# One encoder layer on one core: inverse norms turned into rows on chip, edge factors by memset, score and attention side by side

## The reference

```python
def reference(x, norm1_g, w_in, pool_w, pool_scale, q_norm_g, k_norm_g, sinks,
              w_out, norm2_g, w_up, w_down):
    B, S, _ = x.shape
    for l in range(DEPTH):
        h = rms_norm(x, norm1_g[l])
        proj = jnp.einsum('bsd,de->bse', h, w_in[l])
        u = proj[..., :POOL_WIDTH]
        q = proj[..., POOL_WIDTH:POOL_WIDTH + Q_WIDTH].reshape(B, S, N_Q_HEADS, HEAD_DIM)
        k = proj[..., POOL_WIDTH + Q_WIDTH:POOL_WIDTH + Q_WIDTH + KV_WIDTH].reshape(B, S, N_KV_HEADS, HEAD_DIM)
        v = proj[..., POOL_WIDTH + Q_WIDTH + KV_WIDTH:].reshape(B, S, N_KV_HEADS, HEAD_DIM)
        a = pool_mixer(u, pool_w[l], pool_scale[l])
        b = swa_sink_attention(q, k, v, q_norm_g[l], k_norm_g[l], sinks[l])
        x = x + jnp.einsum('bse,ed->bsd', jnp.concatenate([a, b], axis=-1), w_out[l])
        h2 = rms_norm(x, norm2_g[l])
        hid = jnp.square(jax.nn.relu(jnp.einsum('bsd,df->bsf', h2, w_up[l])))
        x = x + jnp.einsum('bsf,fd->bsd', hid, w_down[l])
    return x
```

## Time and profile before

| what | value |
|---|---|
| median of 3 runs | 887.9 us (887.42 to 890.06) |
| the profiled execution, its own time | 889.13 us |
| its span, first to last instruction | 887.3 us |
| TensorE (PE) busy | 864.1 us, 97% of the span |
| VectorE (DVE), ScalarE (ACT), GpSimd (POOL) busy | 539.1, 407.8, 265.2 us |
| mean granted clock of TensorE | 0.994 of full speed |

### The profile page before, as it was taken

One profiled execution on the slowest core, in us unless ns is written; L12 is line 12 of the kernel. 1 busy time (PEld: TensorE's weight loads), 2 busy tenths in 40 slices (PEclk: granted clock), 3 DMA queues, 4 the chain that ended last, 5 costly groups with the idle time before them and its releaser, 6 DMA issues.

```text
span 887.3 us, 10763 instructions
## 1 busy us (share of the span) xinstructions
PE 864.1 (97%) x4062; PEld 711.1 (80%) x4062; DVE 539.1 (61%) x733; ACT 407.8 (46%) x714; POOL 265.2 (30%) x190
## 2 busy tenths in 40 slices
PE   8797899999999999999999999999999999999998
PEld 7576688678888888888888888888888888888887
DVE  7547856775447766656667656465955464646463
ACT  7346435553225565555555555554333333333330
POOL 1314525201024123432223432002544004444440
PEclk9899999999999999999999999999999999999999
DMA  9362202354110264554344553689762454152522
GB/s 354 54 137 97 60 25 72 82 207 139 48 47 24 86 224 145 184 161 162 131 131 141 186 163 116 212 307 393 271 222 99 149 197 142 59 179 73 165 87 79
DMA packets 69012, 128.90 MB, mean 145 GB/s; under 512 B 4833, under 2 KB 21473, under 8 KB 68961
## 3 DMA queue, kind: packets, MB, share of 16 engines
q1 hardware_dynamic: 68672, 128.08, 43.6%
q10 hardware_dynamic: 288, 0.14, 0.1%
HBM read 90.45 MB, written 37.75 MB: 144 GB/s over the span
## 4 chain that ended last, share of the span: by engine, by line
PE 79%; DMA 7%; DVE 6%; ACT 4%; POOL 2%; issue 1%; SPq 1%; ACTq 0%; DVEq 0%; POOLq 0%
PE bank L1489 26%; PE bank L1490 26%; PE bank L1491 26%; DMA mem<-in_x_T 2%; DMA mem<-in_x 2%; DMA rinv_keep<-mem 1%; DMA d_raw<-in_w_down 1%; DVE ring L1195 1%; PE bank L1502 1%; ACT mem L666 1%; POOL mem L561 1%; DMA raw<-in_w_up 1%; PE bank L1633 1%; DVE h_set L1227 1%; PE bank L1616 1%
## 5 line engine op out<-in xcount | busy, mean ns | idle before, releaser
L1489 PE MATMUL bank<-b_op,s_op 128*128 128x512 f32 (+1 forms) x450 | 174.7, 388 | 0.3 <-DVE b_op L1238 0.3
L1491 PE MATMUL bank<-b_op,s_op 128*128 128x512 f32 (+1 forms) x450 | 174.6, 388 | 0.0
L1490 PE MATMUL bank<-b_op,s_op 128*128 128x512 f32 (+1 forms) x450 | 174.6, 388 | 0.0
L650 POOL TENSOR_TENSOR b_sum<-d_raw,d_raw 128x1024 f32<-128x1024 f32 x40 | 97.7, 2443 | 200.6 <-DVE b_op L1238 200.6
L1234 DVE TENSOR_TENSOR s_op<-s_in,s_op 128x1024 fp32r<-128x1024 f32 x56 | 74.8, 1336 | 124.6 <-ACT s_op L861 124.6
L861 ACT ACTIVATE s_op<-s_in 128x1024 fp32r<-128x1024 f32 x56 | 59.4, 1060 | 177.4 <-PE bank L1491 150.3
L1195 DVE TENSOR_TENSOR ring<-raw,ring 128x512 fp32r<-128x512 f32 x96 | 87.8, 929 | 32.8 <-ACT ring L809 31.8
L1489 PE MATMUL bank<-xs,ring 128*128 128x512 f32 x256 | 99.8, 390 | 0.1
L1490 PE MATMUL bank<-xs,ring 128*128 128x512 f32 x256 | 99.6, 389 | 0.0
L1491 PE MATMUL bank<-xs,ring 128*128 128x512 f32 x256 | 99.6, 389 | 0.0
L1489 PEld LDWEIGHTS bank<-b_op,s_op 128*128 128x128 f32 x450 | 84.5, 188 | 18.2 <-DVE b_op L1238 0.7
(11 more groups left out here) (152 smaller groups left out, 1434.7 us busy)
## 6 DMA issues: line engine op xcount, KB each, us to landing
s_in<-h_keep SPq DMA_DIRECT2D x56, 512.0 KB, 3.9
h_keep<-h_set SPq DMA_DIRECT2D x16, 1280.0 KB, 5.1
raw<-in_w_up SPq DMA_DIRECT2D x16, 1024.0 KB, 6.2
d_raw<-in_w_down SPq DMA_DIRECT2D x32, 512.0 KB, 7.7
mem<-in_x SPq DMA_DIRECT2D x16, 512.0 KB, 6.7
h_keep<-h_set SPq DMA_DIRECT2D x16, 512.0 KB, 3.9
mem<-in_x_T SPq DMA_DIRECT2D x8, 512.0 KB, 7.9
x_keep<-mem SPq DMA_DIRECT2D x8, 512.0 KB, 3.0
```

The costliest lines, as they stand in the source:

```text
L650: nc.gpsimd.tensor_tensor(out=b_sum[G % 2], in0=group_rows(qa, g), in1=group_rows(qb, g), op=op).then_inc(b_summed, 1)
L1489: nc.tensor.matmul(out_ap, lhs[HI], rhs[HI], start=first, stop=False, skip_group_check=chained)
L1490: nc.tensor.matmul(out_ap, lhs[HI], rhs[LO], start=False, stop=False, skip_group_check=chained)
L1491: return nc.tensor.matmul(out_ap, lhs[LO], rhs[HI], start=False, stop=last, skip_group_check=chained)
```

## The change

The column of inverse norms becomes a row without leaving the chip. GpSimd copies the four columns of a half, each along 128 columns, into rinv_row (`spread_rinv`); TensorE transposes the four blocks into the bank QT_B, so that each row of the bank holds the norms of the tokens (`turn_rinv`); ScalarE copies the bank back into rinv_row (`take_rinv`); VectorE's scale_u waits for that. The bank is the one that transpose_in uses, so turn_rinv(h) waits for evac_qk(1) or evac_qk(3) (q_T_ready 2 or 4), and transpose_in(2) and (4) wait for take_rinv. The eight stores, two loads and the HBM tensor go.

The edge factors are written by GpSimd with 30 memsets at the start; VectorE's nine instructions go. On TensorE, the step that stood between score(t+1) and attend(t) is moved behind attend(t) (for attend(1) and attend(5) ahead of the score) at five places. split_w_out(4) is moved back on ScalarE and VectorE, and add_x1(0) is moved ahead of softmax_tail(7) on VectorE.

```diff
@@ -47,7 +47,6 @@
     w_down_i = w_down[0].rearrange("(j i p) n -> i p j n", i=2, p=P)
-    rinv_keep = nc.dram_tensor("rinv_keep", [2, NT // 2, P], F32, kind="Internal").ap()
     x1_keep = nc.dram_tensor("x1_keep", [NT, P, D], F32, kind="Internal").ap()
@@ -180,6 +179,7 @@
         TOK_B = [2, 3, 4, 0]
+        RINV_BEFORE = (2, 4)
@@ -193,7 +193,7 @@
         w_out_in = [sem(f"w_out_in{i}") for i in range(3)]
-        rinv_kept, rinv_row_in = sem("rinv_kept"), sem("rinv_row_in")
+        rinv_spread, rinv_turned, rinv_row_ready = sem("rinv_spread"), sem("rinv_turned"), sem("rinv_row_ready")
         stored = sem("stored")
@@ -333,17 +333,6 @@
                 sp.dma_start(w_u_stage[j], w_u_pair[j][:, :, 0:POOL_W]).then_inc(w_u_in[j], 16)
-
-            def turn_rinv(t):
-                sp.wait_ge(rinv_ready, t + 1)
-                sp.dma_start(rinv_keep[t // KH, t % KH].rearrange("(p i) -> p i", i=1), rinv[:, t:t + 1]).then_inc(rinv_kept, 16)
-
-            def load_rinv_row(h):
-                sp.wait_ge(rinv_kept, 16 * KH * (h + 1))
-                if h:
-                    sp.wait_ge(u_ready, GROUPS)
-                sp.dma_start(rinv_row, rinv_keep[h:h + 1].rearrange("h t p -> h (t p)").to_broadcast([P, HALF])).then_inc(
-                    rinv_row_in, 16)
@@ -413,30 +402,22 @@
             load_x(2)
-            turn_rinv(0)
-            turn_rinv(1)
             load_xT(3)
...
             load_xT(4)
-            turn_rinv(2)
             load_x(4)
-            turn_rinv(3)
             sp.wait_ge(w_u_lo, KT)
...
             sp.wait_ge(w_qkv_lo, KT + 1)
-            load_rinv_row(0)
             load_x(5)
...
                 load_x(t)
-            for t in range(4, NT):
-                turn_rinv(t)
             sp.wait_ge(xT_lo, 2 * (NT - 1))
...
             load_w_out(1)
-            load_rinv_row(1)
             sp.wait_ge(mix_done, GROUPS)
@@ -532,9 +513,10 @@
             pool.wait_ge(setup_pool, 5)
-            nc.gpsimd.iota(edge, [[0, GROUPS], [1, HALO]], base=1, channel_multiplier=0,
-                           allow_small_or_imprecise_dtypes=True).then_inc(setup_pool, 1)
-            pool.wait_ge(setup_pool, 6)
+            for g, w in enumerate(WINDOWS):
+                for j in range(w - 1):
+                    nc.gpsimd.memset(edge[:, g, j:j + 1], w / (j + 1)).then_inc(setup_pool, 1)
+                nc.gpsimd.memset(edge[:, g, w - 1:HALO], 1.0).then_inc(setup_pool, 1)
@@ -544,6 +526,15 @@
                                         op=ALU.pow).then_inc(rinv_ready, 1)
+
+            def spread_rinv(h):
+
+                pool.wait_ge(rinv_ready, KH * (h + 1))
+                if h:
+                    pool.wait_ge(u_ready, GROUPS)
+                column = rinv[:, KH * h:KH * (h + 1)].rearrange("p (t a) -> p t a", a=1)
+                nc.gpsimd.tensor_copy(rinv_row.rearrange("p (t n) -> p t n", n=P),
+                                      column.to_broadcast([P, KH, P])).then_inc(rinv_spread, 1)
@@ -602,6 +593,7 @@
             inverse_rms(3)
+            spread_rinv(0)
             head_squares(2)
@@ -613,6 +605,7 @@
             inverse_rms(7)
+            spread_rinv(1)
             window_sums(0, 3)
@@ -764,6 +757,10 @@
                                      scale=k_gain).then_inc(keys_ready, 1)
+
+            def take_rinv(h):
+                sc.wait_ge(rinv_turned, h + 1)
+                nc.scalar.activation(rinv_row, bank[QT_B][:, :], ACT.Copy).then_inc(rinv_row_ready, 1)
@@ -899,6 +896,7 @@
             evac_probs(0)
+            take_rinv(0)
             x_high(5)
@@ -922,6 +920,7 @@
             evac_probs(2)
+            take_rinv(1)
             copy_kv(4)
@@ -950,12 +949,12 @@
             copy_q(7)
-            split_w_out(4)
             evac_probs(5)
...
             pooled_high(1, 3)
+            split_w_out(4)
             attention_high(5)
@@ -1085,7 +1084,7 @@
                 dve.wait_ge(u_done, n + 1)
-                dve.wait_ge(rinv_row_in, 16 * (h + 1))
+                dve.wait_ge(rinv_row_ready, h + 1)
                 if h:
@@ -1097,6 +1096,8 @@
                 if h == 0:
+                    if g == 0:
+                        dve.wait_ge(setup_pool, 5 + sum(WINDOWS))
                     nc.vector.tensor_copy(u_T[:, g, 0:HALO], u_T[:, g, HALF:UB]).then_inc(halo_ready, 1)
@@ -1249,7 +1250,7 @@
-            dve.wait_ge(setup_pool, 6)
+            dve.wait_ge(setup_pool, 5)
             steps = [0]
@@ -1265,16 +1266,6 @@
                                                  scalar2=None, op0=ALU.mult))
-
-            def window_edges():
-
-                for g, w in enumerate(WINDOWS):
-                    step(nc.vector.tensor_scalar(out=edge[:, g, :], in0=edge[:, g, :], scalar1=float(w), scalar2=None,
-                                                 op0=ALU.min))
-                step(nc.vector.reciprocal(edge, edge))
-                for g, w in enumerate(WINDOWS):
-                    step(nc.vector.tensor_scalar(out=edge[:, g, :], in0=edge[:, g, :], scalar1=float(w), scalar2=None,
-                                                 op0=ALU.mult))
@@ -1309,7 +1300,6 @@
             place_values(1)
-            window_edges()
             head_sums(1)
@@ -1404,8 +1394,8 @@
             attention_low(6)
+            add_x1(0)
             softmax_tail(7)
-            add_x1(0)
             normed_x1(0)
@@ -1571,12 +1561,23 @@
                 pe.wait_ge(qk_ready, t + 1)
+                if t in RINV_BEFORE:
+                    pe.wait_ge(rinv_row_ready, RINV_BEFORE.index(t) + 1)
                 for pr in range(PAIRS):
...
                 nc.tensor.transpose(keys_bank(t), qkv[:, Q_W:Q_W + P], ident).then_inc(kT_done, 1)
+
+            def turn_rinv(h):
+
+                pe.wait_ge(rinv_spread, h + 1)
+                pe.wait_ge(q_T_ready, RINV_BEFORE[h])
+                for i in range(KH):
+                    tok = slice(i * P, (i + 1) * P)
+                    last = nc.tensor.transpose(bank[QT_B][:, tok], rinv_row[:, tok], ident)
+                last.then_inc(rinv_turned, 1)
@@ -1647,30 +1648,30 @@
             transpose_probs(0)
+            turn_rinv(0)
             project_u(0, 1, range(5, KT))
             score(1)
-            project_qkv(3, range(1))
             attend(0)
-            project_qkv(3, range(1, KT))
+            project_qkv(3, range(KT))
             transpose_in(2)
...
             score(2)
-            project_qkv(4, range(1))
+            project_qkv(4, range(2))
             attend(1)
-            project_qkv(4, range(1, 3))
+            project_qkv(4, range(2, 3))
             mix(0, 0)
...
             transpose_probs(2)
+            turn_rinv(1)
             project_qkv(4, range(6, KT))
             score(3)
-            project_qkv(5, range(0, 1))
             attend(2)
-            project_qkv(5, range(1, 4))
+            project_qkv(5, range(4))
             mix(0, 2)
@@ -1688,18 +1689,16 @@
             score(5)
-            project_qkv(7, range(1))
             attend(4)
-            project_qkv(7, range(1, 6))
+            project_qkv(7, range(6))
             transpose_in(6)
...
             transpose_probs(5)
-            project_out(0, range(0, 1))
+            project_out(0, range(0, 2))
             score(6)
             attend(5)
-            project_out(0, range(1, 2))
             mix(1, 2)
```

## The result

The changed kernel takes 872.9 us in the median (871.32 to 872.97, 4 runs), the kernel before 887.73 in the same comparison: a ratio of 0.9823, 95% interval 0.9803 to 0.9843, so 15.7 us less by these ratios. The forecast was 873.5 us, 869 to 879.5.

What follows compares the result with a forecast made beforehand. TensorE, busy 864.1 of 887.3 us, was taken to bound the kernel. The terms summed to 15.1 us, less 0.6 for small waits 14.5: 874.6 us for a profiled execution, 873.5 against the median, range 869 to 879.5.

Steps and rivals of the forecast that it cites:

- why xT(3) is late: Load of x_T's fourth tile: stands behind two 0.5 KB stores that slow everything queued behind them, and takes 11.2 us.
- xT(3) and the first wait: TensorE before 41.78: xT(3) lands in 5 us, so 5.59 us of idle time and 1.73 us of slow clock go.
- Next in line, 1.47 us: TensorE's wait before 58.07: loads and exponentials(0) come earlier, score(1) asks at 49.6, and 1.47 us go.
- The new way of the row: GpSimd's copy takes 1.06 us (bounds 0.5 and 2.1); two turn_rinv on TensorE cost 1.1 us.
- the rival of a held TensorE: TensorE waits 2 to 4 us at turn_rinv(0) for a late release: 877 us, chance 0.13.
- Score(1) to attend(1), 2.83 and 2.21 us: TensorE's waits before 76.86, 78.57 and 89.23: x(5) is issued earlier, so 2.83 and 2.21 us go.
- The third softmax: TensorE's waits of 0.80 and 2.15 us before 98.50 and 101.30: 2.4 us stay, 0.5 us won.
- The half clock: TensorE from 101.30 to 105.47: 1.4 us lost to slow clock, counted at one half, 0.7 us won.
- Adjacent score and attention, 0.8 us: TensorE, five places with a step between score and attention: 0.2 us a place won, four places counted, 0.8 us.
- split_w_out(4) and add_x1(0): Moving split_w_out(4) removes 0.35 us before score(6), w_out(7) landing 4 to 5 us later; add_x1(0) gives nothing.
- The rival of slow loads: xT(3) takes its 11.2 us whatever stands before it, only issued 1.45 us sooner: 881 us, chance 0.10.
- those of no change and of slower: Gain given back between 110 and 200 us: 887 us, chance 0.03; turn_rinv(0)'s wait grown: 891 us or more, 0.02.

Runs made afterwards that it cites:

- e1_word_stores_kept: The changed kernel with the eight stores of 128 neighbouring 4-byte words put back, read by nobody: 886.96 us against 889.8 of the kernel before.
- e2_wide_stores: The changed kernel with eight stores at the old places and with the old waits, each of 128 pieces of 512 bytes: 872.79 us, ratio 0.9806.
- e12: The changed kernel with the eight stores put back as 128 pieces of 64 bytes next to each other: 873.5 us against 890.1 of the kernel before.
- e13: The changed kernel with the eight stores put back as single words 64 bytes apart in HBM: 873.2 us against 888.8 of the kernel before.
- e8_step_between: The changed kernel with TensorE's old order, one step between score and attend, at the five places: 871.95 us, ratio 0.9823.
- e7: The changed kernel with pooled(0,2) moved on VectorE from behind softmax_head(2) to behind softmax_tail(2): 870.32 us, ratio 0.9779.
- e3_row_alone: The kernel before with only the new way of the row, without the edge-factor and order changes: 874.56 us against 889.8, ratio 0.9825.
- e10_tail_reordered: As e7, with attention_low(4) and softmax_head(5) of the first key head moved ahead of head_norm(6) on VectorE: 868.32 us, ratio 0.9757.

## Why the prediction was right, point by point

*What bounds the kernel, and why xT(3) is late.* Right: e1_word_stores_kept shows that the stores alone do it, e2_wide_stores that SyncE's wait, the place in the list and the number of pieces don't. One reading went too far: that the slow landings agree with a rule by the size of the piece. That rule is the Trainium skill's ("DMA: Bandwidth & Descriptors", Specifications): under 512 B a read-modify-write. e12 and e13 show that pieces under 512 bytes, down to single words, cost nothing that can be seen when no two share 64 bytes. The size alone doesn't give this case's times (873.2 to 873.5 us, against 872.8 with 512-byte pieces and 887.0 with neighbouring words); the measurement decides. The rival's rule (the Trainium skill, same page, "Why small descriptors are slow (HBM only)": only a small fixed cost a packet) describes the words apart and not the neighbours. What the chip does inside with neighbouring words was not seen, and whether it is the shared 64 bytes or the short stretch of the whole store stays open.

*xT(3) and the first wait.* Landing was put at 5 us and took 4.7. The 5.59 us went. The clock's share was called 1.73 and was 2.3: from 36.15 to 45.57 the same work took 9.42 us, where I had counted 9.97. Two slips made the difference. transpose_in's five transposes take 0.46 us, as the rows at 36.15 and 36.61 show, not 0.87, which is what the eight of transpose_probs take (45.57 to 46.44). And 0.87 and 39 times 0.228 are 9.76, not 9.97.

*Next in line, 1.47 us.* Right: exponentials(0) and the loads came as said, score(1) at 49.04 where 49.6 was forecast.

*The new way of the row.* GpSimd's copy took 0.61 us, inside the bounds of 0.5 and 2.1. turn_rinv took, by the chain of waits, 0.44 us at full clock (behind 46.44) and 0.76 at half (behind 85.78), 1.2 for both against 1.1 said. Neither waited, so the rival of a held TensorE, put at 0.13, didn't come.

*Score(1) to attend(1), 2.83 and 2.21 us.* Right: both waits are gone, attend(1) at 75.50 where 76.4 was said.

*The third softmax.* Of 0.80 and 2.15 us, 0.5 was expected to go; 0.80 went. The half clock was counted as half gone. In the profiled execution it came in full: the stretch behind the pause took 4.70 us (85.78 to 90.48) where the same work took 3.13 us at full clock (88.67 less 85.54 in e8_step_between). The mean clock was 0.998 in three of four runs of the changed kernel, so nearly nothing of the 0.7 us came. That the products beside GpSimd's sums are the cause was argued there and is shown by e7 for 3.0 of the 3.5 us. The Trainium skill says that GpSimd shares its SBUF interfaces with VectorE and contends with its two-input instructions ("GPSIMD Engine Reference", Specifications). The traces agree: 0.69 us alone, 1.42 and 1.62 beside the sums.

*Adjacent score and attention, 0.8 us.* Wrong, by the count. The 0.2 us a place is there, but of the five places only three put score and attention side by side (attend(0), attend(2), attend(4)), and I took off only the one ahead of 163.67, attend(4). The one at attend(0) lies before a wait that VectorE sets and is lost in it. One is left: from score(3) to the next transpose of keys 12.43 us (90.48 to 102.91) where it was 12.63. So 0.2 us came of 0.8.

*split_w_out(4) and add_x1(0).* The 0.35 us before score(6) went (no wait at 156.49), and nothing was late for the moved split. The changed kernel also has one step more ahead of score(6), but e8_step_between hasn't, and has no wait there either; e3_row_alone, with neither, has the 0.35 us. So the moved split is enough.

*The sum.* The terms as measured in the two profiled executions: 5.59 + 2.28 + 1.47 + 2.83 + 2.21 + 0.80 + 0 + 0.2 + 0.35 - 1.2 = 14.5, against 16.2 of the two spans. Of the other 1.7 us, 0.45 came between transpose_in(2) and score(2), beyond the two waits that went there (the distance of the two timelines grows from 9.22 to 12.50), and 0.3 between the transposes of keys at 163.67 and 180.46, beyond the 0.35; what made these stays open, and the rest lies in stretches too small to name. The mechanism was right, but that the number came out within 0.6 us is in part luck, twice over. Among the terms, a clock term 0.55 too small, a third softmax 0.3 too small and a reserve of 0.6 for new waits that weren't needed (there was only 0.2 us more at the transpose of keys) made good for 0.7 us of clock and 0.6 of order that didn't come. And for an execution like the profiled one 874.6 was said and 872.97 measured, 1.6 us off; the 1.2 us taken off, because the kernel before's profiled execution was slower than its median, closed most of that, though the changed kernel's profiled execution was not slower than its median. The rival of slow loads is refuted by 4.7 us to landing, those of no change and of slower by the result.

## What to carry to other kernels

A store's own bytes say nothing about its price: look at how long the transfers queued behind it take, and ask how its pieces lie in HBM. If a column must be stored to HBM, keep its words apart (64 bytes were enough here; no run loaded such a row back), or turn it on TensorE, which here cost 1.2 us of the bounding engine and won fifteen. When one load chain stops being late, count the gain only up to the next wait that another engine sets (here the softmax beside GpSimd's sums), and move what starts the other engine's work behind what TensorE waits for.

## What the runs showed that was not expected

- 128 neighbouring words stored to HBM, twice, make the 512 KB load behind them take 11 to 12 us; the same words 64 bytes apart leave it at 4.4 us, and so do 128 times as many bytes (3.5 us).
- The clock behind the same pause is not the same in every execution. The changed kernel's profile has 2.15 us of idle time before 85.78, then a granted clock of 0.66 in 85 to 90 us, and 4.70 us until score(3). e2_wide_stores has the same 2.15 us, a clock of 1.00 in 86 to 91 us, and 3.13 us for the same work:

```profile
86.44 0.66 PE L1597 MATMUL bank<-mem 128*128 128x128 f32 x4 [2.15 <-DVE mem L1180]
...
89.57 1.16 PE L1628 MATMUL bank<-mem 64*128 64x128 f32 x16
```

- The changed kernel's own runs fall in two groups for it: 872.9 us in three at a mean clock of 0.998, 871.3 in one at 1.000. With the pause gone (e7) the clock was 1.000 in all five and the times lay within 0.16 us. The clock isn't all of it: e10_tail_reordered, at 1.000 in all four runs, spread over 1.2 us.
